# Last input half of the second feed-forward parts: odd pairs of chunks by seven block products

## The reference

```python
def rmsnorm(x, g):
    y = x * rsqrt(mean(x * x, axis=-1) + EPS)
    return y * g

def swiglu(x, w_in, w_out):
    gate, up = split(x @ w_in, 2, axis=-1)
    return (silu(gate) * up) @ w_out

x = x + 0.5 * swiglu(rmsnorm(x, ffn2_norm[i]), ffn2_w_in[i], ffn2_w_out[i])
```

## Time and profile before

| | |
|---|---|
| median of 3 runs | 2361.28 us (2358.14 to 2363.19) |
| span of the profiled execution | 2357.9 us |
| PE busy | 2332.7 us, 99% |
| DVE busy | 1295.9 us, 55% |
| ACT busy | 869.0 us, 37% |
| POOL busy | 609.4 us, 26% |
| DMA | 289.19 MB, mean 123 GB/s |

### The profile page before, as it was taken

One profiled execution on the slowest core, in us unless ns is written; L12 is line 12 of the kernel. 1 busy time (PEld: TensorE's weight loads), 2 busy tenths in 40 slices (PEclk: granted clock), 3 DMA queues, 4 the chain that ended last, 5 costly groups with the idle time before them and its releaser, 6 DMA issues.

```text
span 2357.9 us, 50146 instructions
## 1 busy us (share of the span) xinstructions
PE 2332.7 (99%) x21043; PEld 2270.3 (96%) x21043; DVE 1295.9 (55%) x1906; ACT 869.0 (37%) x1399; POOL 609.4 (26%) x591
## 2 busy tenths in 40 slices
PE   8999999999999999999999999999999999999999
PEld 8999999889979999999999999999999979999999
DVE  6653643964576443445543344577777666443443
ACT  4422333453233321322433233267775233321323
POOL 4779967331103000004111010432122102000003
PEclk9999999999999999999999999999999999999999
DMA  6455445553562333333543333233332653333332
GB/s 167 128 161 149 123 134 169 171 170 107 166 242 84 98 99 91 96 96 99 158 117 111 100 108 115 83 100 108 104 111 77 213 188 91 97 94 94 98 94 94
DMA packets 483707, 289.19 MB, mean 123 GB/s; under 512 B 22289, under 2 KB 466962, under 8 KB 482514
## 3 DMA queue, kind: packets, MB, share of 16 engines
q1 hardware_dynamic: 477856, 280.66, 40.4%
q0 software_dynamic: 560, 1.84, 0.6%
q10 hardware_dynamic: 5122, 4.25, 0.5%
HBM read 258.86 MB, written 27.85 MB: 122 GB/s over the span
## 4 chain that ended last, share of the span: by engine, by line
PE 90%; DVE 4%; POOL 2%; ACT 1%; issue 1%; DMA 1%; SPq 0%; DVEq 0%; POOLq 0%; ACTq 0%
PE lin L3021 51%; PE lin L3026 25%; PE mis L2512 4%; POOL sTmp L737 1%; PE mis L2650 1%; PE lin L2600 1%; PE lin L2762 1%; PE mis L2633 1%; PE lin L2757 1%; PE lin L2983 1%; POOL sGe L738 0%; DVE w_lo L1827 0%; POOL sFe L738 0%; PE lin L2650 0%; PE mis L2626 0%
## 5 line engine op out<-in xcount | busy, mean ns | idle before, releaser
L1827 DVE TENSOR_TENSOR w_lo<-raw,w_hi 128x1024 fp32r<-128x1024 f32 (+1 forms) x322 | 464.0, 1441 | 294.4 <-ACT w_hi L1330 293.7
L1330 ACT ACTIVATE w_hi<-raw 128x1024 fp32r<-128x1024 f32 (+1 forms) x328 | 365.1, 1113 | 314.2 <-PE lin L3026 244.4
L3021 PE MATMUL lin<-a_rear,w_hi 128*128 128x264 f32 x3552 | 455.6, 279 | 0.0
L3021 PE MATMUL lin<-a_front,w_hi 128*128 128x256 f32 x3552 | 451.5, 279 | 1.1 <-DVE a_rear L1840 0.7
L3021 PEld LDWEIGHTS lin<-a_rear,w_hi 128*128 128x128 f32 x3552 | 432.6, 188 | 0.0
L3021 PEld LDWEIGHTS lin<-a_front,w_hi 128*128 128x128 f32 x3552 | 424.4, 188 | 4.5 <-issue 1.8
L3026 PE MATMUL lin<-a_rear,w_lo 128*128 128x264 f32 x1776 | 245.1, 278 | 0.0
L3026 PE MATMUL lin<-a_front,w_lo 128*128 128x256 f32 x1776 | 240.5, 277 | 1.0 <-DVE w_lo L1827 1.0
L2391 DVE SCALAR_TENSOR_TENSOR xT<-lin,xT 128x520 f32<-128x520 f32 (+1 forms) x87 | 60.9, 700 | 322.8 <-PE lin L3026 322.1
L1063 POOL TENSOR_TENSOR acc<-xT 128x520 f32<-128x520 f32 x8 | 12.2, 1521 | 864.6 <-DVE xT L2391 836.6
L3026 PEld LDWEIGHTS lin<-a_rear,w_lo 128*128 128x128 f32 x1776 | 223.8, 188 | 0.0
(11 more groups left out here) (512 smaller groups left out, 3181.5 us busy)
## 6 DMA issues: line engine op xcount, KB each, us to landing
raw<-in_ffn_w_in_dram SPq DMA_DIRECT2D x176, 512.0 KB, 3.9
raw<-in_ffn_w_out_dram SPq DMA_DIRECT2D x64, 704.0 KB, 4.6
kc<-in_cache_mem_k_dram SPq DMA_DIRECT2D x32, 512.0 KB, 7.1
vc<-in_cache_mem_v_dram SPq DMA_DIRECT2D x16, 1024.0 KB, 9.1
raw<-in_hg_w_in_dram SPq DMA_DIRECT2D x32, 512.0 KB, 4.3
raw<-in_xattn_w_kv_dram SPq DMA_DIRECT2D x16, 512.0 KB, 4.4
raw<-in_s_w_glu_dram SPq DMA_DIRECT2D x16, 512.0 KB, 4.0
raw<-in_xattn_w_q_dram SPq DMA_DIRECT2D x16, 512.0 KB, 3.9
```

The lines of the kernel that those rows point to most:

```text
L1330: act.activation(w_hi[:, j, 0:kt, :], raw[:, j, 0:kt, :], ACT.Copy).then_inc(hi_ready, 1)
L1827: dve.tensor_tensor(low_weights(n, j), raw[:, j, 0:kt, :], w_hi[:, j, 0:kt, :].bitcast(F32), ALU.subtract).then_inc(lo_ready, 1)
L3021: pe.matmul(lpart(j, half), high[:, k, :], (x_lo if u else x_hi)[half][:, k, :], start=start and u == 0 and k == 0, stop=False)
```

## The change

In both layers' ffn2_in1, a pair i with odd i (five of the eleven) is computed by seven block products. The pair's weights are seen as four blocks A11, A12 (chunk 0, weight tiles 0 to 3 and 4 to 7), A21, A22 (chunk 1), the tokens as four blocks B11, B12, B21, B22 (channel tiles 0 to 3 or 4 to 7, tokens in halves of 260, where the first digit is the channel half and the second the token half, counted from the last). DVE forms the sums S1 to S4 of weight blocks and T1 to T4 of token blocks, PE does P1 to P7, 12 products of 260 columns each (4 weight tiles, 3 terms), 84 in all in place of 96, into seven banks, and DVE adds them up (`with_p2_p6`, `with_p5_p7`, `with_p3_p4`). Even pairs are still computed directly, but on the same token blocks of 260 columns.

- The token blocks `mix_hi`, `mix_lo` and the two tiles of the block B12 (`cross`) lie where other stages keep attention's tiles. They carry gain and `rstd`, so the multiplications by `rstd` behind the products go. They are built during ffn2_in0 in `hook`, one channel tile behind each of the pairs 1, 3, 5, 7 (`mixed`, eight DVE operations of 260 elements) and split behind the pairs 2, 4, 6, 8 (one ACT and one DVE operation of 7 x 260 elements). B12 is split in the first pair of ffn2_out0.
- ffn2_in0 and ffn2_in1 are now written out in full on every engine.
- In ffn2_in1 each engine has its own order of work, `seven_products`. SP's loads for an even pair wait for the end of `low_22` of the odd pair before, which raises `lo_ready` by two; the loads for an odd pair follow the two low parts of the even pair before. In an even pair after the first, PE waits for both chunks' parts at the start.
- Two semaphores are joined with others (`hg["lb"]`) and `rows_in` is shortened, since more semaphores are needed.

The core of the diff:

```diff
+                mix["B12"] = cross_raw[:, k, :]
+                for name in ("B11", "B12", "B21", "B22"):
+                    m, cols = k + KQ * (name[1] == "2"), HALVES[name[2] == "1"]
+                    ins = dve.scalar_tensor_tensor(out=mix[name], in0=xT[:, m, cols], scalar=vec[:, row + m:row + m + 1],
+                                                   in1=rstd[:, cols], op0=ALU.mult, op1=ALU.mult)
+                step.link(ins)
+                step.link(dve.tensor_tensor(mix["T1"], mix["B12"], mix["B11"], ALU.subtract))
+                step.link(dve.tensor_tensor(mix["T2"], mix["B22"], mix["T1"], ALU.subtract))
+                dve.tensor_tensor(mix["T3"], mix["B22"], mix["B12"], ALU.subtract)
+                dve.tensor_tensor(mix["T4"], mix["B21"], mix["T2"], ALU.subtract).then_inc(combined, 1)
...
+                    for i in range(FH):
+                        p = first_pair[ST[n][:2]] + i
+                        for e, j in enumerate(chunk_order(i - 1) if by_seven(i) else (0, 1)):
+                            column, src = weights(n, i, j)
+                            sp.wait_ge(lo_ready, 2 * p + e - 1)
+                            sp.dma_start(raw[:, j, 0:KD, :], src[:, :, bass.ds(column, P)]).then_inc(raw_arrived[j], 16)
```

ACT's order in ffn2_in1 (`high_second` copies chunk 1's weights, `high_22` the block A22, `high_sums` two of the sums):

```diff
+                for i in range(FH):
+                    p, s_ = p0 + i, SEVENS * layer + i // 2
+                    if by_seven(i):
+                        hidden_hi(i - 1)
+                        act.wait_ge(product_done, 4 * s_ + 1)
+                        act.activation(rows[:, ROW_P1], bank_p1, ACT.Copy).then_inc(product_kept, 1)
+                        for j in chunk_order(i + 1):
+                            if j:
+                                high_second(p + 1)
+                            else:
+                                split(p + 1, 0, n)
+                        continue
+                    if i:
+                        act.wait_ge(used[0], p)
+                        act.activation(rows[:, ROW_SILU], rows[:, ROW_GATE], ACT.Silu).then_inc(gate_out, 1)
+                        hidden_hi(i - 1)
+                    else:
+                        split(p, 1, n)
+                    if i < FH - 1:
+                        high_sums(s_, 0)
+                        high_sums(s_, 1)
+                    split(p + 1, 0, n if i < FH - 1 else n + 1)
+                    if i < FH - 1:
+                        high_22(p + 1)
+                    act.wait_ge(chunk_done, 2 * p + 1)
+                    act.activation(rows[:, ROW_SILU], lin[:, 0, :, 0:HT], ACT.Silu).then_inc(used[0], 1)
```

DVE's order (`first_sum` is S1, `other_sums` S2 to S4, `low_sums` the low parts of two sums, `low_11` that of chunk 0, `low_22` that of A22):

```diff
+                    if by_seven(i):
+                        gated_chunk(i - 1)
+                        low_chunk(p + 1, chunk_order(i + 1)[0], 1)
+                        hidden_lo(i - 1)
+                        u2 = with_p2_p6(s_)
+                        low_chunk(p + 1, chunk_order(i + 1)[1], 2)
+                        with_p5_p7(s_, u2)
+                        continue
+                    more = i < FH - 1
+                    if i:
+                        with_p3_p4(p - 1)
+                    else:
+                        low_chunk(p, 1, 2)
+                    if more:
+                        s1 = first_sum(p + 1)
+                    if i:
+                        gated_rows(i - 1)
+                    if more:
+                        other_sums(p + 1, s_, s1)
+                        low_sums(s_, 0)
+                    if i:
+                        hidden_lo(i - 1)
+                    if more:
+                        low_11(p + 1)
+                        low_22(p + 1)
+                        low_sums(s_, 1)
```

PE, start of an odd pair and waits of an even one:

```diff
+                def seven_of(p, s_):
+                    pe.wait_ge(hi_ready, 2 * p + 1)
+                    wait(pe, product_kept, s_)
+                    high(bank_p1, a1_hi[:, 0:KQ], "B11")
+                    pe.wait_ge(first_low, s_ + 1)
+                    low(bank_p1, a1_lo[:, 0:KQ], "B11").then_inc(product_done, 1)
+
+                    pe.wait_ge(used[0], p)
+                    high(bank_p2, a1_hi[:, KQ:KD], "B21")
+                    low(bank_p2, a1_lo[:, KQ:KD], "B21").then_inc(chunk_done, 1)
...
+                def eight_of(p, i):
+                    if i == 0:
+                        pe.wait_ge(combined_low, parts_of_tokens(layer, CROSS))
+                        pe.wait_ge(hi_ready, 2 * p + 1)
+                        pe.wait_ge(used[0], p)
+                    else:
+                        pe.wait_ge(hi_ready, 2 * p + 2)
+                        pe.wait_ge(lo_ready, 2 * p + 2)
```

More of the change, by code:

```diff
@@ L55, in link, with mark, after @@
         self.eng.wait_ge(self.sem, self.off + self.n)
+    def mark(self, ins):
+        ins.then_inc(self.sem, 1)
+        self.n += 1
+        return self.off + self.n
+    def after(self, mark):
+        self.eng.wait_ge(self.sem, mark)
     def loop(self, i, first, per):
@@ L511, in over_pairs, with by_seven, chunk_order, seven @@
         body(p0 + pairs - 1, pairs - 1, False, True)
+    SEVENS = FH // 2
+    def by_seven(i):
+        return i % 2 == 1
+    def chunk_order(i):
+        return (1, 0) if 0 < i < FH - 1 else (0, 1)
+    def seven(n):
+        return n < len(ST) and ST[n][0] == "ffn2_in1"
+    def of_tokens(layer, k):
+        return (KQ + 2 * SEVENS) * layer + k + 1
+    def of_weights(s_, pair):
+        return (KQ + 2 * SEVENS) * (s_ // SEVENS) + KQ + 2 * (s_ % SEVENS) + pair + 1
+    CROSS = KQ
+    def parts_of_tokens(layer, k):
+        return (KQ + 1 + 2 * SEVENS) * layer + k + 1
+    def parts_of_weights(s_, pair):
+        return (KQ + 1 + 2 * SEVENS) * (s_ // SEVENS) + KQ + 1 + 2 * (s_ % SEVENS) + pair + 1
+    MIX_RAW = {("ffn2_in0", l, 1 + 2 * k): k for l in range(DEPTH) for k in range(KQ)}
+    MIX_SPLIT = {("ffn2_in0", l, 2 + 2 * k): k for l in range(DEPTH) for k in range(KQ)}
     def chunk_after(n, j, last):
@@ L541, in gate_base @@
     def gate_base(n):
-        per = {"ffn1_in0": FH, "ffn1_in1": FH, "ffn2_in0": FH, "ffn2_in1": FH, "hg_in": 2 * HH}
+        per = {"ffn1_in0": FH, "ffn1_in1": FH, "ffn2_in0": FH, "ffn2_in1": SEVENS, "hg_in": 2 * HH}
         return sum(per.get(s_[0], 0) for s_ in ST[:n])
@@ L1753, in body @@
                             split(p + 1, 0, chunk_after(n, 1, last))
+                        if first and j == 1 and seven(n + 1):
+                            act.activation(cross_hi[:], cross_raw[:], ACT.Copy).then_inc(combined_high, 1)
                         if after is not None and is_out(name):
@@ L1764, in stream, with seven_products, high_second, high_22 @@
                 over_pairs(act, n, body, hook)
+            def seven_products(n):
+                p0, layer = first_pair[ST[n][:2]], ST[n][1]
+                def high_second(p):
+                    act.wait_ge(raw_arrived[1], 16 * (p + 1))
+                    act.wait_ge(chunk_done, 2 * (p - 1))
+                    act.activation(w_hi[:, 1, 0:KD, :], raw[:, 1, 0:KD, :], ACT.Copy).then_inc(hi_ready, 1)
+                def high_22(p):
+                    act.wait_ge(raw_arrived[1], 16 * (p + 1))
+                    act.activation(sum_hi[:, SUMS["A22"]], raw[:, 1, KQ:KD, :], ACT.Copy).then_inc(hi_ready, 1)
+                def high_sums(s_, pair):
+                    act.wait_ge(combined, of_weights(s_, pair))
+                    blocks = slice(2 * pair, 2 * pair + 2)
+                    act.activation(sum_hi[:, blocks], sum_raw[:, blocks], ACT.Copy).then_inc(combined_high, 1)
+                def hidden_hi(i):
+                    act.wait_ge(used[1], p0 + i + 1)
+                    for out, cols in zip(f_hi, COLS):
+                        ins = act.activation(out[:, i, :], hidden_row[:, cols], ACT.Copy)
+                    ins.then_inc(h_hi_done, 1)
+                for i in range(FH):
[24 more added lines that the diff above has]
+                    act.activation(rows[:, ROW_SILU], lin[:, 0, :, 0:HT], ACT.Silu).then_inc(used[0], 1)
+                hidden_hi(FH - 1)
@@ L1770, in _ @@
                     hg_in()
+                    continue
+                if seven(n):
+                    seven_products(n)
                     continue
@@ L1834, in split_part, with mixed @@
                                          ALU.subtract)
+            def mixed(layer, k):
+                if k == 0:
+                    dve.wait_ge(kv_vout, 16 * (layer + 1))
+                row = NORM_ROW[norm_of["ffn2_in0", layer]]
+                mix = {name: mix_raw[:, b, k, :] for name, b in COMBOS.items()}
+                mix["B12"] = cross_raw[:, k, :]
[8 more added lines that the diff above has]
+                dve.tensor_tensor(mix["T4"], mix["B21"], mix["T2"], ALU.subtract).then_inc(combined, 1)
             def gain_lo(m, r):
@@ L1999, in hook @@
                 at_ = (name, layer, i)
+                if at_ in MIX_RAW:
+                    mixed(layer, MIX_RAW[at_])
+                if at_ in MIX_SPLIT:
+                    k_ = MIX_SPLIT[at_]
```

(9 more changed lines are left out.)

193 lines of the change are left out of this document (185 added, 8 removed).

## The result

The change makes the kernel slower. Its median is 2366.77 us (2361.83 to 2371.08) against 2359.58 us (2357.20 to 2364.06) of the kernel before on the same chips; the ratio is 1.0030, 95% interval 1.0022 to 1.0038, so 7.2 us. The profiled span is 2364.4 us where it was 2357.9. The forecast was 2357.1 with a range of 2353.5 to 2364.5: the measured time lies outside it, and the sign was wrong.

The account below looks back on a forecast made before the run. PE time was taken to bound the kernel. Per layer 6.9 + 0.3 - 4.4 - 0.45 - 0.1 = 2.25 us; both 4.5, less 0.3 in ffn2_in0, gave 4.2 off 2361.3: 2357.1 us, range 2353.5 to 2364.5.

Parts of the forecast that it names:

- Step (a), the price of a product: ffn2_in1: 260 columns cost 115.0 ns, so odd pairs take 9.66 us instead of 11.04; 13.8 us saved over both layers.
- dearer products: Rival: products on the new tiles in ffn2_in1 always cost 5.5 ns more, giving 2365.0 us; chance 0.10.
- Step (c), the start: Start of ffn2_in1, around the first odd pair: PE gaps of 1.16, 0.34 and 2.9 us, 4.4 us per layer.
- The clock: the rival: Rival: granted clock drops in the gap at ffn2_in1's start, 1.75 us per layer, 1.3 net, giving 2359.7; chance 0.22.
- Step (d), the ring: ffn2_in1's steady pairs: loads, ACT and DVE from one `low_22` to the next take 20.85 us, PE 20.70; 0.45 per layer lost.
- Step (e), mixed code: Odd pairs in ffn2_in1: PE loses time changing between banks and weight sources, 0.1 us per layer, bounds 0 to 0.29 x 5.
- Step (f), ffn2_in0: ffn2_in0: added DVE and ACT work for the token blocks delays PE by 0.04 x 8 = 0.3 us.
- right at 7.33: ffn2_in0, work added at pairs 2, 4, 6, 8: DVE's split ends at 7.3 us, PE wants it at 7.33.
- smaller start: Rival: loads land within 5.7 us and DVE is quicker; ffn2_in1's start gaps total 3.5 us per layer, 2354.3; chance 0.08.

Follow-up runs that it names:

- pitch 1152 and the new order: Changed kernel with token tiles at pitch 1152, and ACT and DVE doing the first odd pair's splits and low parts ahead of sums: 2357.55 us, ratio 0.9992.
- The version with 264 columns: Changed kernel with pitch 1152, reordered start, a direct pair's loads in order of use, and 264-column products in ffn2_in1: 2351.16 us, ratio 0.9963.

## Why the prediction was wrong

- **Step (a), the price of a product: this is the step that failed, and it decides the sign.** "A product of 260 columns should take 260/2.4 + 6.7 = 115.0 ns" interpolated between two widths, each of which had been seen in one sequence only. It is 120.0, so 5.0 us per layer and 10.0 us in all; the saving of 13.8 became 3.8. Why 260 columns in these tiles cost 120.0 stays open beyond the two conditions that the runs show, the pitch and the sequence. The rival *dearer products* named the place, the sign and the size (5.5 ns, 2365.0) but had a chance of 0.10, and its cause, the pitch, is only part of it: at pitch 1152 and 260 columns 118.9 to 119.8 remain. That its total fits is in part luck, since the clock drops came on top and the gaps were smaller. The earlier trace rows were the sign of it that the trace of before held: the same instruction at 121 instead of 116.7. They show that columns / 2.4 GHz + 6.7 holds in some sequences only; the prediction used them for the rival and not for the price itself.
- **Step (c), the start: right in mechanism and nearly in size.** Gaps of 1.12, 0.30 and 2.68 us against 1.16, 0.34 and 2.9; in layer 1 0.94, 0.30 and 2.12. Released by ACT's `w_hi` and DVE's `w_lo`, as said. The chain was worked at 115 ns a product; PE's slower pace (0.5 us over pair 0, 0.4 us over pair 1) shortens the gaps, while the load that the first sum waits for landed 7.9 us into the stage and not 7.4. A load's time to landing, put at 5.1 us, was 5.0 to 7.3 for the same load in three runs, which moves these gaps from execution to execution.
- **The clock: the rival was the case,** at both places, for 1.35 and 1.60 us against 1.75. The forecast held that an idle time between 2.33 and 2.85 us would keep it since full products follow at once. Here 2.53 us and even 1.97 lost it, and 2.33 in another place kept it. At the gap before pair 2 of the other runs 2.12 and 2.13 us kept it and 2.27 and more lost it. And the idle time of 2.85 us that lost it in the earlier trace rows recurs, to within 0.01 us, at the same place in ten other traces: eight lost the clock, two kept it, as here with 264 columns everywhere in ffn2_in1 (granted clock 1.00):
```profile
196.75 0.65 PE L2874 MATMUL mis<-sGe,bZ 128*32 128x128 f32 x16 [2.85 <-POOLq L1277]
...
197.00:200.00 3.00, 3.00 (x46) 2.97 (x37) 0.00 (x0) 1.54 (x2) 2.72 (x3) 1.00 1.07 208
```
So between 1.97 and 2.85 us neither the length of the idle time nor the work around it decides alone. The prediction's argument from full products isn't borne out, and what does decide these traces don't tell. The Trainium skill, "TensorE: Matmul & The Clock Gate", "Part 1: The HAM clock gate", has throttled as the default that activity lifts, and the trace agrees as far as it goes: behind both idle times products ran at 217 ns before they ran at 120 again.
- **Step (d), the ring: hidden.** No idle time before pairs 4, 6, 8. This doesn't show that its 20.85 us were right: at 120.0 ns PE itself needs 96 + 84 products, 21.6 us a round, and covers it. With pitch 1152 and the new order PE needs 21.4 and shows no gap there either, so the ring is at most that. The version with 264 columns needs 21.0 without a gap, but its loads go out in another order, so it says nothing of this ring.
- **Step (e), mixed code: nothing to be seen**; at 264 columns the stage of layer 1 is its products and no more.
- **Step (f), ffn2_in0: mis-sized.** Instead of 0.3 us for both layers it was 0.41 and 0.44. In each layer the pairs 3, 5, 7 and 9 lose 0.07 us or a little more at the low weights; that is 0.3 of the 0.4 us, the rest was not followed:
```profile
836.26 1.98 PE L3424 MATMUL lin<-a_front,w_hi 128*128 128x256 f32 x16
838.07 1.16 PE L3429 MATMUL lin<-a_front,w_lo 128*128 128x256 f32 x8
839.07 2.03 PE L3424 MATMUL lin<-a_rear,w_hi 128*128 128x264 f32 x16
```
The eight from 838.07 to 839.07 take 1.00 us and not 0.91. It is the place that the prediction named, "right at 7.33".
- **The base of the forecast was misread.** It takes the 3.4 us between the span of 2357.9 and the median of 2361.3 for "start and end around it". In every execution on record the time exceeds its own span by 1.7 to 2.3 us; the rest is the difference between executions. The median of 13 executions of the kernel before is 2359.58, so the same gain of 4.2 us would have been about 2355.4, further from what was measured. The rival *smaller start* has a slip too: its gaps of 1.0, 0.3 and 2.3 add up to 3.6, and its 2354.3 takes in that the ring's 0.9 us go, which it doesn't say.

With the measured sizes in its own sum: span 2353.7 + 10.0 (a) + 2.95 (clock) - 1.3 (smaller gaps) - 0.9 (ring) - 0.2 (e) + 0.55 (f) + 0.45 (restarts) - 0.8 (rest of the program) = 2364.4, the span measured. The structure of the sum held. What failed was to give the largest factor, 1992 products, a price without bounds; the two rivals that came true together had been given 0.10 and 0.22, each by itself.

## What to carry to other kernels

Where a change keeps the work but alters the width or the tile of a product that runs two thousand times, its price per product is the first unknown and not a matter of interpolation: 5 ns each cancelled 10 of 13.8 us saved. Measure the new width in the new tile and in the new sequence, try padding up to a width known to be clean (264 columns were quicker than 260), and take any stretch of the old trace where the same instruction is slower as a bound. At a stage's start look for queues in which work that PE wants now stands behind work that it wants later; putting it ahead here was worth 7 us, a part of that because the idle times left, 1.31 us and less, kept the clock.

## What the runs showed of the hardware

- The time of a product of 256 columns, unchanged itself, went from 113.3 to 117.8 ns because half of the products around it went from 264 to 256 columns.
- With the rear tiles at pitch 1088, the same products of 256 columns, in the same tiles and sequence, took 117.7 ns in ffn2_in0 and 113.8 in ffn2_in1, in both layers.
- Tiles 1088 bytes apart instead of 1152 made 24 products of 264 columns take 2.90 us instead of 2.80, and made the kernel before some 39 us slower.
- At pitch 1152, 272 columns took 126.6 ns and 264 took 116.7: eight columns for 10 ns, where 8 / 2.4 GHz is 3.3.
- The granted clock fell to its 1.2 GHz level behind idle times of 1.97 and 2.53 us and stayed at 2.4 GHz behind 1.31 us. Behind 2.85 us at one and the same place it fell in nine traces and stayed in two.
